# A decoder block with routed experts: the second token tile's block attention moved beside the gathers, its index logits behind the attention units, and the first conditioning pieces loaded in halves

## The reference, cut to what matters

```python
mod = silu(c) @ ada_w + ada_b                  # conditioning: shift, scale, gate, twice
h = rms_norm(x) * (1 + scale1) + shift1
z = h @ W_in
# NSA, 8 query heads: compressed blocks + selected blocks + window, each with a gate
k_cmp, v_cmp = compress_blocks(kc), compress_blocks(vc)       # gelu MLP on 15 blocks
o_cmp = masked_softmax(q @ k_cmp.T * scale) @ v_cmp           # the block attention
# DSA, 8 query heads: an indexer scores all keys, the best 64 are kept
score = sum_h(w_h * relu(qi_h @ ki.T * scale)); sel = top_k(score, 64)   # index logits
x = x + gate1 * ((sig(g_nsa) * (o_nsa @ W_nsa) + sig(g_dsa) * (o_dsa @ W_dsa)) @ W_out)
h = rms_norm(x) * (1 + scale2) + shift2
# PEER: 8 heads, 16 experts for each token and head out of 16384
e = top_k(product keys(h @ wq)); x = x + gate2 * sum(gate * gelu(h . u[e]) * v[e])
return rms_norm(x)
```

## Time and profile before

| | before |
|---|---|
| median of 3 runs | 981.22 us (981.1 to 983.23) |
| profiled execution | 977.82 us |
| its span | 976.0 us |
| mean granted TensorE clock | 0.957 |
| PE busy | 800.7 us (82%) |
| DVE busy | 645.1 us (66%) |
| ACT busy | 409.1 us (42%) |
| POOL busy | 283.5 us (29%) |
| gathers (q0) | 268.45 MB, 66.5% of 16 engines |
| other transfers (q1) | 73.31 MB, 18.9% of 16 engines |

### The profile page before, as it was taken

One profiled execution on the slowest core, in us unless ns is written; L12 is line 12 of the kernel. 1 busy time (PEld: TensorE's weight loads), 2 busy tenths in 40 slices (PEclk: granted clock), 3 DMA queues, 4 the chain that ended last, 5 costly groups with the idle time before them and its releaser, 6 DMA issues.

```text
span 976.0 us, 9734 instructions
## 1 busy us (share of the span) xinstructions
PE 800.7 (82%) x2940; PEld 445.9 (46%) x2940; DVE 645.1 (66%) x1663; ACT 409.1 (42%) x1148; POOL 283.5 (29%) x260
## 2 busy tenths in 40 slices
PE   4899969999888989887787788697777778777775
PEld 3644557888873544444454354232322222222221
DVE  4521446996359897886766866867858667586644
ACT  4101132223246887633243634544544344343433
POOL 0000000000033544453343435354253442534420
PEclk8699979998999999999999999999899999999998
DMA  9982403768049999999999999999999999999993
GB/s 373 424 332 92 173 1 111 321 259 344 24 170 424 412 419 419 373 422 418 420 418 419 421 419 420 422 420 422 422 422 421 422 422 421 421 422 422 420 422 125
DMA packets 46899, 342.84 MB, mean 351 GB/s; under 512 B 5312, under 2 KB 6528, under 8 KB 10624
## 3 DMA queue, kind: packets, MB, share of 16 engines
q0 software_dynamic: 36864, 268.45, 66.5%
q1 hardware_dynamic: 9536, 73.31, 18.9%
q10 hardware_dynamic: 448, 0.46, 0.2%
HBM read 341.16 MB, written 1.05 MB: 351 GB/s over the span
## 4 chain that ended last, share of the span: by engine, by line
DMA 45%; PE 27%; DVE 14%; ACT 6%; issue 4%; POOL 2%; SPq 0%; DVEq 0%; POOLq 0%
DMA extra<-in_uv,arena 27%; DMA arena<-in_uv,arena 9%; PE banks L470 7%; DMA ring<-in_uv,arena 7%; PE banks L711 6%; PE banks L504 5%; DVE extra L1480 3%; DMA extra<-in_w_ada 3%; PE banks L664 1%; DVE arena L1480 1%; PE banks L653 1%; PE banks L683 1%; ACT L1002 1%; ACT extra L1012 1%; PE banks L587 1%
## 5 line engine op out<-in xcount | busy, mean ns | idle before, releaser
L711 PE MATMUL banks<-extra 128*128 128x512 f32 x500 | 243.5, 620 | 59.3 <-ACT extra L1012 59.2
L802 POOL DMA_INDIRECT extra<-in_uv,arena x136 | 152.2, 1119 | 459.4 <-DVE arena L1463 315.0
L1002 ACT ACTIVATE arena<-arena 128x1 f32<-128x1 f32 x256 | 51.7, 202 | 323.8 <-DVE arena L1480 323.3
L711 PE MATMUL banks<-arena,extra 128*128 128x512 f32 x296 | 149.1, 633 | 40.0 <-ACT extra L1012 40.0
L711 PEld LDWEIGHTS banks<-extra 128*128 128x128 f32 x500 | 88.7, 193 | 193.5 <-ACT extra L1012 113.9
L1480 DVE CUSTOM_DVE_ANT_0 extra<-extra 128x1024 f32<-128x1024 f32 x80 | 97.9, 1227 | 51.1 <-DMA extra<-in_uv,arena 49.9
L802 POOL DMA_INDIRECT arena<-in_uv,arena x80 | 86.2, 1078 | 129.4 <-PE banks L711 56.4
L711 PEld LDWEIGHTS banks<-arena,extra 128*128 128x128 f32 x296 | 52.9, 196 | 126.9 <-ACT extra L1012 83.7
L1012 ACT ACTIVATE extra<-tab,arena 128x128 f32<-128x128 f32 x235 | 94.3, 401 | 7.7
L1480 DVE CUSTOM_DVE_ANT_0 extra<-extra,arena 128x1024 f32<-128x1024 f32 x56 | 68.6, 1225 | 42.4 <-DMA extra<-in_uv,arena 41.7
L711 PE MATMUL banks<-ring,extra 128*128 128x512 f32 x144 | 73.6, 638 | 26.0 <-ACT extra L1012 26.0
(11 more groups left out here) (242 smaller groups left out, 1064.8 us busy)
## 6 DMA issues: line engine op xcount, KB each, us to landing
arena<-in_w_ada SPq DMA_DIRECT2D x8, 2048.0 KB, 12.1
arena<-in_w_late SPq DMA_DIRECT2D x24, 512.0 KB, 8.3
extra<-in_w_ada SPq DMA_DIRECT2D x4, 2048.0 KB, 10.3
arena<-in_w_in SPq DMA_DIRECT2D x3, 2048.0 KB, 27.4
extra<-in_w_gate SPq DMA_DIRECT2D x3, 2048.0 KB, 8.3
extra<-in_w_br SPq DMA_DIRECT2D x2, 2048.0 KB, 13.9
arena<-in_w_wq SPq DMA_DIRECT2D x2, 2048.0 KB, 18.6
extra<-in_uv,arena POOLq DMA_INDIRECT x136, 18.9
```

The costliest lines, as they stand in the source:

```text
L711: last = nc.tensor.matmul(acc[tt][:, half * 512:(half + 1) * 512], diag[i % DIAGS], uv_slot[SLOT[v]][:, D + half * 512:D + (half + 1) * 51 ...
L802: nc.gpsimd.indirect_dma_start(uv_slot[SLOT[g]], None, A["uv"], bass.IndirectOffsetOnAxis(ap=expert[:, g:g + 1], axis=0)).then_inc(uv_in[S ...
L1002: link(nc.scalar.activation(gel[:, v:v + 1], dots[:, v:v + 1], ACT.Gelu))
```

## The change

The first four conditioning pieces are loaded in two halves with a semaphore for the first; ACT and DVE begin on the first half, and for piece 3 DVE adds the two partial sums so that PE multiplies one. The compressed hidden row goes ahead of the index logits on DVE, and its tanh ahead of the last two head copies on ACT. Index logits 4 to 7 move from before the units to behind them. The block attention is cut into functions; the second tile's part now runs in the gather loop at g = 1 to 14, and `vbd` is made twice. Head 0's scores go ahead of query(0, 1) on PE; ACT's loop over queries and heads is not changed. The pieces of the diff stand in the order SP, PE, ACT, DVE.

```diff
-AT_X1ROW, AT_G2ROW, AT_OUT0 = 117, 128, 143
+AT_BLK, AT_X1ROW, AT_G2ROW, AT_OUT0 = 1, 117, 128, 143
+        vcmp = wukv[:, 0:DH]
+        logit_bank = [B[0], B[1], B[2], B[3], B[2], B[3], B[2], B[3]]
+        cs_bank, pct_bank = [B[0], B[4]], [B[2], B[4]]
+        logit_relu = [relu[0], relu[1], relu[0], relu[1], ssb[0], ssb[1], ssb[0], ssb[1]]
...
+                if kind == "ada" and m < 4:
+                    half = WCOLS // 2
+                    sp.dma_start(dst[:, 0:half], src[:, 0:half]).then_inc(ada_in[m], 16)
+                    dst, src = dst[:, half:], src[:, half:]
                 sp.dma_start(dst, src).then_inc(w_in[SLOT_OF[n]], 16)
...
-                        for i in range(2):
+                        for i in range(1 if m == 3 else 2):
...
+            def logits(q):
+                if q == 3:
+                    pe.wait_ge(fill_out, 1)
+                if q >= 6:
+                    pe.wait_ge(relu_done, q - 1)
+                for i in range(2):
+                    last = nc.tensor.matmul(logit_bank[q][:, i * ns:(i + 1) * ns], q_tile[tt][:, QI + 2 * hp + i, :],
...
+            def block_turn(tt):
+                pe.wait_ge(pc_ready, tt + 1)
+                nc.tensor.transpose(pct_bank[tt][0:HEADS * NCMP, 0:P], pc[:, tt, :], ident).then_inc(pct_done, 1)
+            def block_output(tt):
+                pe.wait_ge(pct_ready, tt + 1)
+                pe.wait_ge(vbd_ready, tt + 1)
...
-            for q in range(8):
+            for q in range(4):
+                logits(q)
             pe.wait_ge(hid_ready, 1)
...
             gate(1)
-            pe.wait_ge(cmpkv_ready, 2)
-            pe.wait_ge(relu_done, 8)
-            for tt in range(TT):
+            pe.wait_ge(cmpkv_ready, 1)
+            pe.wait_ge(relu_done, 4)
+            block_scores(0)
             gate(2)
+            block_turn(0)
             gate(3)
+            block_output(0)
...
+            logits(4)
+            logits(5)
             turn_outputs(0)
+            logits(6)
+            logits(7)
             for m in range(KT):
                 branch(0, m)
...
-            for m in range(KT + 1):
+            query(0, 0)
+            head_scores(0, 0)
+            for m in range(1, KT + 1):
                 if m < KT:
                     query(0, m)
-                if m:
+                if m >= 2:
                     head_scores(0, m - 1)
...
+                if g == AT_BLK:
+                    block_scores(1)
+                if g == AT_BLK + 2 * BEHIND:
+                    block_turn(1)
+                if g == AT_BLK + 3 * BEHIND + 1:
+                    block_output(1)
...
-                w = chunk(act, "ada", m).rearrange("p (k n) -> p k n", k=KT)
+                act.wait_ge(ada_in[m], 16)
...
-            for n in range(8, len(JOBS)):
+            for n in range(8, len(JOBS) - 2):
+                job_copy(n)
+            act.wait_ge(hid_in, 1)
+            nc.scalar.activation(hid[:, 120:180], hid[:, 120:180], ACT.Tanh, scale=float(np.sqrt(2.0 / np.pi))).then_inc(tanh_done, 1)
+            for n in range(len(JOBS) - 2, len(JOBS)):
                 job_copy(n)
...
             open_gates(0)
+            logit_copy(4)
+            logit_copy(5)
             turn_copies(0)
+            logit_copy(6)
+            logit_copy(7)
             open_gates(1)
...
+                if g == AT_BLK + BEHIND:
+                    block_exp(1)
+                if g == AT_BLK + 3 * BEHIND:
+                    block_copy(1)
...
                 for k in range(2, KT):
+                    if k == 4:
+                        chunk(dve, "ada", m)
...
+                if m == 3:
+                    dve.wait_ge(dve_step, steps[0])
+                    ins = V.tensor_tensor(ada_part[1][0], ada_part[1][0], ada_part[1][1], ALU.add)
                 ins.then_inc(ada_summed, 1)
...
+            for q in range(4):
+                score_add(q)
+            dve.wait_ge(cmpkv_done, 1)
+            V.tensor_copy(kcmpT, B[7][0:DH, P:P + 2 * NCMP]).then_inc(cmpkv_ready, 1)
+            link(V.tensor_copy(vcmp[0:rows, :], B[7][0:rows, T:T + DH]))
+            block_values()
+            block_max(0)
+            block_norm(0)
+            block_sum(0)
...
             dve.wait_ge(fill_done, 16)
+            for q in range(4, 8):
+                score_add(q)
             for i in range(4):
                 select(1, 2 * i)
...
+                if g == AT_BLK + BEHIND:
+                    block_max(1)
+                if g == AT_BLK + BEHIND + 1:
+                    block_values()
+                if g == AT_BLK + 2 * BEHIND - 1:
+                    block_norm(1)
+                if g == AT_BLK + 4 * BEHIND + 1:
+                    block_sum(1)
```

115 lines of the change are left out of this document (56 added, 59 removed).

## The result

The changed kernel's median is 978.65 us (969.19 to 981.69, 20 runs) where the kernel before, run beside it on the same chip, has 981.86. The ratio is 0.9946 with an interval of 0.9926 to 0.9965: a gain of about 5.3 us, 3.4 to 7.3. Forecast was 12.2, with a range that ended at 975.5. A second series of the same kernel gave 975.91 (969.63 to 985.04, 12 runs), ratio 0.9937 [0.9902, 0.9973]. The sign was right and the size was not. The executions of the changed kernel lie in two groups, 969 to 974 and 976 to 985. The record has the mean granted clock of each execution: in the quicker group it is 0.953 (second series 0.954), in the slower one 0.946 (0.943). Over a span of 976 us this difference is worth an estimated 6.4 us (10.2) of TensorE at full speed, and the groups' mean times differ by 7.7 us (9.9).

The account below looks back on a forecast made before the run. DMA gathers near 420 GB/s were taken as a full pipe, so their start and gaps set the time. Terms -2.6 - 11.8 - 0.65 + 0.65 + 2.2 = -12.2 gave 969.0 us from the 981.22 median; range 963.5 to 975.5.

Parts of the forecast that it names:

- units: The twelve units: bound by PE in both kernels with the same instructions, so 0 us.
- Two loads: Conditioning pieces in two loads: PE's projection starts sooner, -2.6 us, ends -3.3 and -1.5.
- Compression ahead: Ahead of the first unit: compression before the logits, -11.8 us net of 1.7 for half clock, ends -13.5 and -10.5.
- Rival 1: Ahead of the logits: the clock holds over the 2.3 us idle, -13.9 us, 967.3; chance 0.15.
- rival 6: ACT's table changes: the page's drain comes on both tables, -9.5 us, 971.7; chance 0.02.
- Logits behind the units: Units' end to branch: idle filled, branch at full clock, -0.65 us, ends -0.8 and +1.7.
- Head 0's scores: Ahead of query(1): ACT's head copy and the first gather come later, +0.65 us, ends 0 and +1.
- Block attention beside the gathers: First gathers: added work on DVE, ACT and PE frees slots late, +2.2 us, ends +0.3 and +4.5.
- rival 4: Gather loop: each unit makes PE idle, then half clock, 1.6 us for each of twelve units; +7, 988; chance 0.05.
- Rival 3: Gathers lose 4.5 to 8 us, ACT having little to spare; -10 to -6.4, 971 to 975; chance 0.12.
- signs of being wrong: Units starting later than 147, DVE's score additions pushing the first merge, or the stream losing more than 4.5 us.

Follow-up runs that it names:

- r5: The changed kernel with all four last head copies ahead of the tanh on ACT; 972.59 us, ratio 0.9922.
- r18: The changed kernel with tanh last, head scores back behind the next query, and full matmuls at three places (six, seven, four); 968.16 us, ratio 0.9855.
- r12: The changed kernel with block attention back before the units, head scores back behind the next query, and tanh last; 969.77 us, ratio 0.9899.
- r15: r12 with six extra full matmuls around the logits behind the units; 970.29 us, ratio 0.9875.
- r16: r15 with ten more full matmuls ahead of the first value step; 967.25 us, ratio 0.9852.
- r7: The changed kernel with logits 4 to 7 back ahead of the units, and unused 64-row matmuls in their place behind them; 987.5 us, one execution.
- r6: The changed kernel with the block attention's exponential one gather later, behind a unit's exponential; 976.80 us, ratio 0.9967.
- r13: The changed kernel with block attention back before the units, and VectorE's share of it done a second time at gathers 4 to 14; 978.74 us, one execution.
- r1: The changed kernel again with no edit, the second series; 975.91 us, ratio 0.9937.
- r9: The changed kernel with ten extra full matmuls behind head 7's scores, ahead of the first value step; 973.12 us, ratio 0.9892.

## Why the prediction was wrong, step by step

The steps, in us against before, by the profiles of after, of its second series and of the versions:

| step | predicted | after | second series | the version with less half clock there |
|---|---|---|---|---|
| two loads, at the projection | -2.6 | -3.1 | -3.0 | |
| from there to the first unit | -11.8 | -8.4 | -12.2 | -14.5 (r5, tanh last) |
| units | 0 | 0 | +0.3 | 0 |
| units' end to mix_out | -0.65 | +5.6 | +5.25 | -0.9 (r5) |
| mix_out to query(0) | 0 | 0 | 0 | 0 |
| query(0) to the first gather | +0.65 | +2.1 | +0.6 | +0.65 (r5) |
| gathers to the end | +2.2 | +7.0 | +4.6 | +4.5 (r18) |
| sum | -12.2 | +3.3 | -4.4 | |

**Two loads.** Right in mechanism and within its ends: the addition took the 0.69 us, the eight instructions 1.87. One thing was missed: "the gain arrives whole at the next stage" did not hold. The half clock at the start of the projection ended only 1.35 us sooner (40.12 for 41.47) where the projection began 3.1 us sooner, so the earlier start bought 0.9 us more of it, and at 110 us the shift is 2.2. That is contained in the second row.

**Compression ahead.** The path is the one that was summed: PE waits 2.38 us (2.3 predicted) for the two late job copies, and the logits, products and gates follow in the predicted order. The term that was mis-sized is the clock: 1.7 us by an idle of like length. The second series has 1.7 on gate(1) (5.41 for 3.72) and starts units at 143.28, for 144.1 predicted. The first profile has 4.8 (3.63 for 2.05, 1.07 for 0.72, 6.63 for 3.72) and starts at 147.04. The row that I borrowed the price from has full 128-row products behind its idle; here 64-row logits follow, and the half clock lasted 10.2 us in one execution and 3.4 in the other. That the 64 rows are the cause here was not tested apart. Rival 1 (the clock holds over the idle) did not come true in either profile. Nor did rival 6: the table load at 122.70 takes 1.28 us and the tanh starts at 124.00. Taking most of the idle away shortens the half clock but doesn't exclude it: ahead of the units it lasts 3.4 to 17 us in the fourteen profiles with 2.38 us of idle, and 0 (r5), 3.4 (r12, r15, r16) and 6.8 us (r18) in the five with 0.82.

**Logits behind the units.** This step failed, and it is the largest miss, 6 us: "With the idle filled I expect it at full clock". Its premise was that the branch began at half clock because of the idle, and the rows of before already speak against it: the clock fell 0.5 us into an idle of 1.48. In after it fell at the same place, and lasted 13.7 us, over logits, turn and the branch's start, where before has 6.8; the end that I named, +1.7, was too small for that. The branch starts 4.6 us later behind the units' end than before, where 0.6 would do at full clock (r5), and takes 1.0 us longer. That the clock is what costs is shown by r5: the same instructions at full clock take 21.1 us instead of 27.6. That full products bring it back sooner than 64-row ones is shown by r18 against r7. VectorE's additions went into its wait for the branch as predicted: mix_out follows the branch by the same 1.75 us idle.

**Head 0's scores.** Right where the half clock there is as long as before, 3.4 us (+0.6 in the second series and in r5), 2.1 where it is 6.8 us and reaches over query(1).

**Block attention beside the gathers.** Of +7.0 and +4.6 the stream's loss makes nearly all (10.6 and 8.0 against 3.4). With the clock held all through the first gathers (r18) the loss is 6.5, 3.1 over before, and the time behind the first gather 4.5 longer: both inside the predicted 0.3 to 4.5, so the +2.2 was too small by 1 to 2 us for the lateness alone. At the turn and the output product for which the prediction had PE wait (gathers 7 and 11) TensorE doesn't idle in after and r5. The further 1 to 5 us fit half clock behind two idles, ahead of the first value step and ahead of the value product at gather 10; by single profiles this is likely and not shown. The prediction had the second mechanism in rival 4, from the earlier trace rows, with a price of 1.6 us for each of twelve units and the point "from eight units on". It doesn't come through unit by unit: in the first 160 us of gathers the clock falls four times in after and five times in before, and beyond them nothing more is lost. Rival 3 (the gathers lose 4.5 to 8) is what came true for this term, with a chance of 0.12; its reason, that ScalarE has no slack, was only half of it (r6: nothing gained by 2.6 us less ScalarE; r13: VectorE alone 7.6).

**The range.** It summed ends of each term as if they were independent, but four of the five terms have one common part, the clock, and in the first profile it went against me in all of them. The sum of the named ends was also taken short: they add up to -17.3 and -4.8, which from 981.2 is 963.9 to 976.4, still below 978.65. With what the first profile has in place of these ends (-8.4, +5.6, +2.1, +7.0) the sum lies at 985. Of the signs of being wrong that the prediction named, the units' start is at its bound (147.04 and 143.28 for 147), VectorE's additions did not push the merges, and the stream loses 7.2 and 4.6 us more than before, for a bound of 4.5.

What stays open: why the clock falls at the end of the units at all, and why it held there in r5 and fell in the second series, with the same instructions. The two groups of executions differ in their mean clock by about what they differ in time, but only one execution of each series has a profile, so where the slower ones lose it isn't shown.

## What to carry to other kernels

When an edit moves or fills work on TensorE, ask of what kind the matmuls are that will stand beside an idle or in its place: products with 64 rows kept the engine busy here and did not bring its clock back, and full 128x128 products in their place did so within 3.4 us or kept it. Price each stretch at both clocks, and put the slow ends of all steps together in the range, since they come together. And before work is moved beside a stream of transfers, look for the first place where the engine that feeds it waits for DMA again: the same share of VectorE and ScalarE cost 7 us of stream at gathers 4 to 14 and nothing at 24 to 34, in one profile each.

## What of the hardware was not expected

TensorE was busy without a break behind the units, the granted clock was 0.50, and it stayed there for 13.7 us over products with 64 rows (r7) and for 3.4 us over products with 128 rows (r18). The clock fell at the end of the units with no idle to bring it about: 0.8 us (r1) and 1.7 us (r9) before the last unit product had ended, with the engine busy. The same kernel stayed at half clock for 10.2 us behind one idle of 2.38 us in one execution and for 3.4 us behind the same idle in another. And the mean clock of an execution tells its group: 0.953 and 0.954 in the quick ones of the two series, 0.946 and 0.943 in the others.
